# A two-block transformer kernel on one core: the first 256-column product of each one-bank quantum becomes two products of 128 columns

## The chip, the cores and the metric

The kernel runs on 1 core of one Trainium2 chip. The metric is the device time of one execution in microseconds (us), the median of the runs made.

## What is computed

The reference runs three layers over one sequence of 256 tokens of width 1024, all in float32, and returns the tokens:

- layer 1, a gated linear recurrence: `proj = rms_norm(h) @ a_w_in` (1024 by 4096, split into q, f, i, g), a recurrence over chunks of 64 frames, a gate, `@ a_w_out`, then a squared-relu MLP `relu(h @ w_up)**2 @ w_down` (1024 by 4096 and back);
- layer 2, differential attention: `kv = rms_norm(h) @ w_kv` (1024 by 2048), `q = rms_norm(h) @ w_q`, two softmaxes for each of 8 heads whose difference weighs the values, `@ b_w_out`, and a second such MLP;
- layer 3, a mixer: `z = rmsnorm(x) @ w_in_2` (2080 columns, cut into a low-rank q and kv, a rotary key and three gates), causal attention, a gated short convolution, `@ w_out_2`, a gated feed-forward of width 2816 and a last gated addition.

Every projection is a matrix product of the 256 tokens with a weight matrix. These products are nearly all of TensorE's work.

## The kernel before, in words

The program is written out by hand, engine by engine. Each engine runs its own list of instructions and waits on semaphores.

**Weights.** SyncE loads weights in parts of 128 partitions by 1024 float32 values into `w_raw` (4 buffers). ScalarE rounds each part to the float32r type in `w_hi` (line 1426, 5 slots), and VectorE writes the remainder `w_raw - w_hi` to `w_lo` (line 1993, which raises `lo_ready`). The activations are held in the same way: `xs[:, kt, 0:256]` is the rounded part of the 256 tokens for the 128 input features kt, and `xs[:, kt, 256:512]` is the remainder. `xs_b` and `us` are further buffers of that layout. One float32 product is three float32r products: high by high, remainder of x by high, and high by remainder of w.

**Units and quanta.** A unit is 256 output columns by 1024 input rows, that is two parts. A quantum is the work on one part: 4 groups of 128 input rows (`kk`) by 2 output halves (`n`) by 3 products, 24 products in all. The first eight quanta of the program have two groups of rows and so 12 products. `quantum` writes them in one of five kinds, which differ in where the sums stand in PSUM:

- `feat` (lines 644 to 665): the streams of the big projections, with some products of 512 columns;
- `direct` and `tok` (lines 676 to 678 and 695 to 697): the last pair of such a stream;
- `one_bank` (lines 682 to 684): both halves in one PSUM bank, weights stationary, tokens moving;
- `one_bank_tok` (lines 689 to 691): the same with tokens stationary and weights moving, so the result has tokens on the partitions.

**Where one-bank quanta stand.** In three places, and nowhere else:

1. the input projection of layer 1 ("the first stage"): 8 quanta of 12 products and then 28 of 24, the loop `for q in range(4, HGRN_QUANTA)`. After most of them stands a piece of the recurrence (`use`, lines 904 to 936): plain float32 products, scores of 128, 64 or 32 columns;
2. keys, values and queries of layer 2 ("the second stage"): 20 quanta of 24, `diff_quantum`, with `scores` (line 1038) and transposes (line 1046) between them;
3. the mixer's projections ("the third stage"): 12 quanta of 24, `narrow`, with the attention of layer 3 between them (lines 1205 to 1230).

Each quantum first waits for `lo_ready` of its part and, with its last product, gives the slot free (`w_used`).

A plain float32 product is one instruction of the program and two records of the trace, each with its own weight load. A float32r product is one record with one weight load. `keep_streaming` (line 826) issues plain float32 products of 256 columns to bridge a pause.

Of the kernel before, what the change touches and what calls it, by code (L numbers as in the profile page):

```python
# [17 lines left out]
P = 128  # L18
D = 1024
S = 256  # L20
# [208 lines left out]
def layered_kernel(nc, a, out):  # L229

    ctx = ExitStack()
    with ctx:
# [122 lines left out]
        ps = ctx.enter_context(nc.psum_tensor("ps", [P, 8, 512], F32))  # L355
# [244 lines left out]
        def _(pe):  # L600
            mm = nc.tensor.matmul
# [39 lines left out]
            def quantum(s, kt0, nk, last_kt, x, kind, pset, kk0=0, tiles=(0, 1), wide=0, wide_first=False):  # L641

                hi, lo = w_hi[:, s, :].rearrange("p (k n) -> p k n", k=4), w_lo[:, s, :].rearrange("p (k n) -> p k n", k=4)
                if kind == "feat":
                    steps = [(kk, n) for kk in range(kk0, kk0 + nk) for n in tiles]

                    def both_halves(some):
                        for kk, n in some:
                            o = mm(ps[:, 2 * pset + n, :], hi[:, kk, n * P:(n + 1) * P], x[:, kt0 + kk, :],  # L649
                                   start=kt0 + kk == 0, stop=kt0 + kk == last_kt)  # L650
                        return o

                    def one_half(some):
                        for kk, n in some:
                            for half in range(2):
                                at = slice(half * S, (half + 1) * S)
                                mm(ps[:, 2 * pset + n, at], hi[:, kk, n * P:(n + 1) * P], x[:, kt0 + kk, at], start=False,  # L657
                                   stop=False)
                        for kk, n in steps:
                            o = mm(ps[:, 2 * pset + n, 0:S], lo[:, kk, n * P:(n + 1) * P], x[:, kt0 + kk, 0:S], start=False,  # L660
                                   stop=False)
                        return o

                    if wide_first:
                        both_halves(steps[:wide])
                        return one_half(steps[wide:])
                    one_half(steps[:-wide])
                    return both_halves(steps[-wide:])
                for kk in range(kk0, kk0 + nk):
                    kt = kt0 + kk  # L670
                    first, last = kt == 0, kt == last_kt
                    for n in tiles:
                        bank = 2 * pset + n
                        if kind == "direct":
                            w = slice(n * P, (n + 1) * P)
                            mm(ps[:, bank, 0:S], hi[:, kk, w], x[:, kt, 0:S], start=first, stop=False)  # L676
                            mm(ps[:, bank, 0:S], hi[:, kk, w], x[:, kt, S:2 * S], start=False, stop=False)  # L677
                            o = mm(ps[:, bank, 0:S], lo[:, kk, w], x[:, kt, 0:S], start=False, stop=last)  # L678
                        elif kind == "one_bank":
                            w = slice(n * P, (n + 1) * P)  # L680
                            at = slice(n * S, (n + 1) * S)
                            mm(ps[:, pset, at], hi[:, kk, w], x[:, kt, 0:S], start=first and n == 0, stop=False)  # L682
                            mm(ps[:, pset, at], hi[:, kk, w], x[:, kt, S:2 * S], start=False, stop=False)  # L683
                            o = mm(ps[:, pset, at], lo[:, kk, w], x[:, kt, 0:S], start=False, stop=last and n == 1)  # L684
                        elif kind == "one_bank_tok":
                            xh = x[:, kt, n * P:(n + 1) * P]
                            xl = x[:, kt, S + n * P:S + (n + 1) * P]
                            at = slice(n * S, (n + 1) * S)
                            mm(ps[:, pset, at], xh, hi[:, kk, :], start=first and n == 0, stop=False)  # L689
                            mm(ps[:, pset, at], xh, lo[:, kk, :], start=False, stop=False)  # L690
                            o = mm(ps[:, pset, at], xl, hi[:, kk, :], start=False, stop=last and n == 1)
                        else:
                            xh = x[:, kt, n * P:(n + 1) * P]
                            xl = x[:, kt, S + n * P:S + (n + 1) * P]
                            mm(ps[:, bank, 0:S], xh, hi[:, kk, :], start=first, stop=False)
                            mm(ps[:, bank, 0:S], xh, lo[:, kk, :], start=False, stop=False)
                            o = mm(ps[:, bank, 0:S], xl, hi[:, kk, :], start=False, stop=last)
                return o

            def first_two(name, x, waits, mid=None):  # L700

                u, p = UNIT0[name], PAIR0[name]
                wait(pe, pair_summed, p)
                for b, k2 in ((0, 0), (0, 1), (1, 0), (1, 1), (0, 2), (0, 3), (1, 2), (1, 3)):
                    part = k2 // 2
                    if (b, k2) == (1, 0):
                        pe.wait_ge(unit_taken, HGRN_QUANTA // 2)
                    if b == 1 and k2 == 2 and mid is not None:
                        mid()
                    pe.wait_ge(lo_ready, 2 * (u + b) + part + 1)  # L710
                    if b == 0:
                        waits(2 * k2, 2)
                    o = quantum((2 * (u + b) + part) % SLOTS, 4 * part, 2, KT - 1, x, "feat", (p + b) % 2,
                                kk0=2 * (k2 % 2), wide=WIDE[2 * part + b][k2 % 2], wide_first=k2 % 2 == 0)

                    if b == 0 and k2 % 2:
                        o.then_inc(w_used, 1)
                    elif (b, k2) == (1, 3):
                        o.then_inc(w_used, 2)
# [9 lines left out]
            def split_unit(u, kt0, last_kt, x, kind, pset, between_tiles=None):  # L729

                for n in range(2):
                    if n == 1 and between_tiles is not None:
                        between_tiles()
                    for part in range(2):
                        nk = min(4, last_kt + 1 - kt0 - 4 * part)
                        o = quantum((2 * u + part) % SLOTS, kt0 + 4 * part, nk, last_kt, x, kind, pset, tiles=(n,))
                        if n == 1:
                            o.then_inc(w_used, 1)
                        elif part == 1:
                            o.then_inc(tail_done, 1)  # L740
# [224 lines left out]
            for q in range(4, HGRN_QUANTA):  # L965
                n, part = q // 2, q % 2
# [158 lines left out]
            for part in range(2):  # L1125
# [3 lines left out]
                for kk in range(4):  # L1129
                    kt = 4 * part + kk  # L1130
# [53 lines left out]
            for m in range(2):  # L1184
                if m == 1:
                    pe.wait_ge(z_dve, BY_DVE["uq3"])
                for kt in range(2):
                    s = (2 * UNIT0["ukv"] + kt) % SLOTS
                    xh, xl = (xs_s[:, 2 + kt, S * i + m * P:S * i + (m + 1) * P] for i in range(2))
# [115 lines left out]
            for b, k2 in ((0, 0), (0, 1), (1, 0), (1, 1), (0, 2), (0, 3), (1, 2), (1, 3)):  # L1305
# [6 lines left out]
                if b == 0:  # L1312
                    out2_wait(2 * k2, 2)
                o = quantum((2 * (u + b) + part) % SLOTS, 4 * part, 2, KT - 1, xs_m, "feat", (p + b) % 2,
                            kk0=2 * (k2 % 2), wide=WIDE[2 * part + b][k2 % 2], wide_first=k2 % 2 == 0)
# [1746 lines left out]
```

## Time and profile before

| | us |
|---|---|
| median of 3 runs | 964.85 |
| lowest and highest run | 964.24 and 965.42 |
| the profiled execution's own time | 964.67 |
| its span | 962.8 |
| TensorE busy in the span | 951.4 (99%), 7530 products |
| weight loads busy | 910.4 (95%), 7530 loads |
| VectorE busy | 747.8 (78%) |
| ScalarE busy | 547.8 (57%) |
| granted TensorE clock | 1.00, that is 2.4 GHz |

The span is what the trace covers; the execution's own time is 1.9 us longer. A product's record lasts from its start to the end of its results, and the next product starts well before that. So the pace of the products is read from the distance of their starts, or from the busy time of a group divided by its count, and not from the length of one record. In the tables below, PE is TensorE's product side, PEld its weight loads, DVE is VectorE, ACT is ScalarE and POOL is GpSimd.

### The profile page before, as it was taken

To read this page: it belongs to the slowest core of one execution; us is meant where nothing else is said; L and a number is where in the kernel's file an instruction comes from. 1 tells how busy PE (TensorE), PEld (TensorE's weight loads), DVE (VectorE), ACT (ScalarE), POOL (GpSimd) and SP (SyncE) were. 2 spreads that over 40 slices of the span, in tenths; PEclk is the share of its full clock that TensorE was granted. 3 is DMA by queue.
4 is the path that set the end of the run, shared out by engine and by line. 5 is a ranking of instruction groups with operands and counts; after the bars stand their busy time and mean duration, and the time that the engine had idled before them with its cause. 6 is when DMAs were issued, how large, how long until landed. Compare 5 with 4: busy or idle time off the path is not lost.

```text
span 962.8 us, 18424 instructions
## 1 busy us (share of the span) xinstructions
PE 951.4 (99%) x7530; PEld 910.4 (95%) x7530; DVE 747.8 (78%) x1129; ACT 547.8 (57%) x813; POOL 89.4 (9%) x91
## 2 busy tenths in 40 slices
PE   9999999999999999999999999999999999999998
PEld 8999999999999999999999999999999999999998
DVE  7898778978855599867987845489887998787776
ACT  6642366656454476666666534455566665556454
POOL 5334101000201000001000201001001000000000
PEclk9999999999999999999999999999999999999999
DMA  8743444766666836435566565626536366655651
GB/s 257 241 122 116 145 126 139 217 199 198 190 186 195 259 118 212 136 119 178 150 204 204 171 214 189 186 77 182 178 112 211 111 202 214 191 183 178 197 173 44
DMA packets 164723, 166.62 MB, mean 173 GB/s; under 512 B 6784, under 2 KB 162832, under 8 KB 164640
## 3 DMA queue, kind: packets, MB, share of 16 engines
q1 hardware_dynamic: 162752, 163.47, 54.6%
q0 software_dynamic: 1056, 1.19, 0.5%
q10 hardware_dynamic: 832, 0.79, 0.4%
q8 instruction: 60, 0.98, 0.4%
q14 instruction: 23, 0.19, 0.1%
HBM read 163.82 MB, written 1.08 MB: 171 GB/s over the span
## 4 chain that ended last, share of the span: by engine, by line
PE 80%; DVE 13%; issue 2%; ACT 2%; DMA 2%; SPq 0%; POOL 0%; ACTq 0%; DVEq 0%
PE ps L657 19%; PE ps L660 16%; PE ps L649 13%; DVE w_lo L1993 4%; PE ps L682 2%; PE ps L676 2%; PE ps L678 2%; PE ps L677 2%; PE ps L683 2%; PE ps L684 2%; PE ps L609 2%; PE ps L617 2%; PE ps L610 2%; PE ps L689 1%; PE ps L690 1%
## 5 line engine op out<-in xcount | busy, mean ns | idle before, releaser
L1993 DVE TENSOR_TENSOR w_lo<-w_raw,w_hi 128x1024 fp32r<-128x1024 f32 (+4 forms) x314 | 374.9, 1204 | 116.8 <-ACT w_hi L1426 111.0
L1426 ACT ACTIVATE w_hi<-w_raw 128x1024 fp32r<-128x1024 f32 x298 | 313.4, 1056 | 200.5 <-PE ps L660 47.6
L657 PE MATMUL ps<-xs,w_hi 128*128 128x256 f32 x1012 | 133.1, 277 | 0.0
L657 PEld LDWEIGHTS ps<-xs,w_hi 128*128 128x128 f32 x1012 | 127.4, 188 | 4.5
L660 PE MATMUL ps<-xs,w_lo 128*128 128x256 f32 x832 | 112.6, 277 | 0.0
L660 PEld LDWEIGHTS ps<-xs,w_lo 128*128 128x128 f32 x832 | 103.2, 188 | 0.2
L682 PE MATMUL ps<-xs,w_hi 128*128 128x256 f32 x320 | 91.4, 286 | 0.0
L683 PE MATMUL ps<-xs,w_hi 128*128 128x256 f32 x320 | 89.4, 280 | 0.0
L684 PE MATMUL ps<-xs,w_lo 128*128 128x256 f32 x320 | 89.4, 279 | 0.0
L649 PE MATMUL ps<-xs,w_hi 128*128 128x512 f32 x326 | 85.3, 393 | 0.2 <-DVE mo L2021 0.2
L1433 ACT ACTIVATE tmp<-ps 128x512 f32<-128x512 f32 x75 | 44.6, 595 | 71.2 <-PE ps L649 63.0
L657 PE MATMUL ps<-us,w_hi 128*128 128x256 f32 x626 | 81.8, 277 | 0.0
L657 PEld LDWEIGHTS ps<-us,w_hi 128*128 128x128 f32 x626 | 78.6, 188 | 2.8
L2021 DVE TENSOR_TENSOR mo<-ps,tmp 128x512 f32<-128x512 f32 x75 | 51.5, 687 | 37.8 <-ACT tmp L1433 37.8
L2971 POOL TENSOR_TENSOR sq<-sq 128x512 f32<-128x512 f32 x12 | 20.1, 1678 | 545.8 <-ACT sq L1484 375.2
L660 PE MATMUL ps<-us,w_lo 128*128 128x256 f32 x516 | 69.3, 277 | 0.0
L649 PEld LDWEIGHTS ps<-xs,w_hi 128*128 128x128 f32 x326 | 56.6, 188 | 9.9 <-DVE mo L2021 1.6
L660 PEld LDWEIGHTS ps<-us,w_lo 128*128 128x128 f32 x516 | 63.6, 188 | 0.0
L682 PEld LDWEIGHTS ps<-xs,w_hi 128*128 128x128 f32 x320 | 60.1, 188 | 0.9 <-issue 0.3
L683 PEld LDWEIGHTS ps<-xs,w_hi 128*128 128x128 f32 x320 | 60.1, 188 | 0.2
L684 PEld LDWEIGHTS ps<-xs,w_lo 128*128 128x128 f32 x320 | 60.0, 187 | 0.0
L649 PE MATMUL ps<-us,w_hi 128*128 128x512 f32 x203 | 53.4, 394 | 0.0
(431 smaller groups left out, 1892.0 us busy)
## 6 DMA issues: line engine op xcount, KB each, us to landing
w_raw<-in_mlp_w_up SPq DMA_DIRECT2D x64, 512.0 KB, 4.1
w_raw<-in_mlp_w_down SPq DMA_DIRECT2D x64, 512.0 KB, 3.7
w_raw<-in_a_w_in SPq DMA_DIRECT2D x32, 512.0 KB, 4.4
w_raw<-in_w_gate SPq DMA_DIRECT2D x22, 512.0 KB, 3.9
w_raw<-in_w_up SPq DMA_DIRECT2D x22, 512.0 KB, 4.5
w_raw<-in_w_down SPq DMA_DIRECT2D x20, 512.0 KB, 4.1
w_raw<-in_w_kv SPq DMA_DIRECT2D x16, 512.0 KB, 4.3
w_raw<-in_w_in SPq DMA_DIRECT2D x16, 512.0 KB, 4.0
```

Source lines behind the costliest of these rows:

```text
L609: mm(o_ap, hi[:, w], x[:, kt, 0:S], start=kt == 0 and (kind == "feat" or n == 0), stop=False)
L649: o = mm(ps[:, 2 * pset + n, :], hi[:, kk, n * P:(n + 1) * P], x[:, kt0 + kk, :], start=kt0 + kk == 0, stop=kt0 + kk == last_kt)
L657: mm(ps[:, 2 * pset + n, at], hi[:, kk, n * P:(n + 1) * P], x[:, kt0 + kk, at], start=False, stop=False)
L660: o = mm(ps[:, 2 * pset + n, 0:S], lo[:, kk, n * P:(n + 1) * P], x[:, kt0 + kk, 0:S], start=False, stop=False)
L682: mm(ps[:, pset, at], hi[:, kk, w], x[:, kt, 0:S], start=first and n == 0, stop=False)
L683: mm(ps[:, pset, at], hi[:, kk, w], x[:, kt, S:2 * S], start=False, stop=False)
L684: o = mm(ps[:, pset, at], lo[:, kk, w], x[:, kt, 0:S], start=False, stop=last and n == 1)
L1426: o = fn(dst, raw, ACT.Copy)
L1433: o = fn(tmp[0:rows_, pset if slot is None else slot, :, :], ps[0:rows_, 2 * pset:2 * pset + 2, S:2 * S], ACT.Copy, scale=scale)
L1993: return v.tensor_tensor(d, x, y, ALU.subtract)
L2021: return v.tensor_tensor(dst, ps[0:rows_, 2 * pset:2 * pset + 2, 0:S], tmp[0:rows_, pset if slot is None else slot, :, :], ALU.add)
L2971: g.tensor_tensor(pair(j), pair(j), pair(j - 1), ALU.add).then_inc(sq_added, 1)
```

## The change

In `one_bank` and `one_bank_tok`, the very first product of a quantum (first group of rows, half 0, high by high) is issued as two products of 128 columns, each with the same stationary operand and one half of the moving columns. The flag that opens the accumulation stands on the first of the two alone. All other products stay as they are.

```diff
                         elif kind == "one_bank":
                             w = slice(n * P, (n + 1) * P)
                             at = slice(n * S, (n + 1) * S)
-                            mm(ps[:, pset, at], hi[:, kk, w], x[:, kt, 0:S], start=first and n == 0, stop=False)
+                            if kk == kk0 and n == 0:
+                                for m in range(2):
+                                    half = slice(m * P, (m + 1) * P)
+                                    mm(ps[:, pset, half], hi[:, kk, w], x[:, kt, half], start=first and m == 0, stop=False)
+                            else:
+                                mm(ps[:, pset, at], hi[:, kk, w], x[:, kt, 0:S], start=False, stop=False)
                             mm(ps[:, pset, at], hi[:, kk, w], x[:, kt, S:2 * S], start=False, stop=False)
                             o = mm(ps[:, pset, at], lo[:, kk, w], x[:, kt, 0:S], start=False, stop=last and n == 1)
                         elif kind == "one_bank_tok":
                             xh = x[:, kt, n * P:(n + 1) * P]
                             xl = x[:, kt, S + n * P:S + (n + 1) * P]
                             at = slice(n * S, (n + 1) * S)
-                            mm(ps[:, pset, at], xh, hi[:, kk, :], start=first and n == 0, stop=False)
+                            if kk == kk0 and n == 0:
+                                for m in range(2):
+                                    half = slice(m * P, (m + 1) * P)
+                                    mm(ps[:, pset, half], xh, hi[:, kk, half], start=first and m == 0, stop=False)
+                            else:
+                                mm(ps[:, pset, at], xh, hi[:, kk, :], start=False, stop=False)
                             mm(ps[:, pset, at], xh, lo[:, kk, :], start=False, stop=False)
                             o = mm(ps[:, pset, at], xl, hi[:, kk, :], start=False, stop=last and n == 1)
```

On TensorE the program has 7203 product instructions before and 7271 after, 68 more: one for each of the 8 + 28 + 20 + 12 quanta. No other engine's list changes. In the first stage, after a piece of the recurrence, TensorE's list before reads:

```order
L684 MATMUL ps<-xs,w_lo 128x256
L936 MATMUL ps<-hq_both,hk 128x64 x8
L682 MATMUL ps<-xs,w_hi 128x256
L683 MATMUL ps<-xs,w_hi 128x256
L684 MATMUL ps<-xs,w_lo 128x256
L682 MATMUL ps<-xs,w_hi 128x256
```

and now:

```order
L689 MATMUL ps<-xs,w_lo 128x256
L946 MATMUL ps<-hq_both,hk 128x64 x8
L685 MATMUL ps<-xs,w_hi 128x128 x2
L688 MATMUL ps<-xs,w_hi 128x256
L689 MATMUL ps<-xs,w_lo 128x256
L687 MATMUL ps<-xs,w_hi 128x256
```

The first product behind the recurrence's eight is now two of half the width (line 685); line numbers behind the edit are 5 higher here, and 10 higher below both edits. Where the tokens are stationary, TensorE's list before is:

```order
L926 MATMUL ps<-hq_both,hk 32x32 x16
L689 MATMUL ps<-w_hi,xs 128x256
L690 MATMUL ps<-w_lo,xs 128x256
L691 MATMUL ps<-w_hi,xs 128x256
L689 MATMUL ps<-w_hi,xs 128x256
```

and now:

```order
L936 MATMUL ps<-hq_both,hk 32x32 x16
L697 MATMUL ps<-w_hi,xs 128x128 x2
L700 MATMUL ps<-w_lo,xs 128x256
L701 MATMUL ps<-w_hi,xs 128x256
L699 MATMUL ps<-w_hi,xs 128x256
```

Again one product of 256 columns has become two of 128 (line 697), and the rest stands as before.

## Rows read from the trace of the kernel before

**Rows 1.** The page: busy times, clock, and the chain that ended last by engine.
```profile
PE 951.4 (99%) x7530; PEld 910.4 (95%) x7530; DVE 747.8 (78%) x1129; ACT 547.8 (57%) x813; POOL 89.4 (9%) x91
...
PEclk9999999999999999999999999999999999999999
...
PE 80%; DVE 13%; issue 2%; ACT 2%; DMA 2%; SPq 0%; POOL 0%; ACTq 0%; DVEq 0%
```

**Rows 2.** Timeline of PE, first stage, 41 to 55 us: start, length, what.
```profile
41.92 1.97 PE L917 MATMUL ps<-hq_both,hk 128*128 128x128 f32 x16
43.65 0.37 PE L682 MATMUL ps<-xs,w_hi 128*128 128x256 f32 x1
...
51.74 0.28 PE L683 MATMUL ps<-xs,w_hi 128*128 128x256 f32 x1
51.86 0.28 PE L684 MATMUL ps<-xs,w_lo 128*128 128x256 f32 x1
...
52.33 1.89 PE L936 MATMUL ps<-hq_both,hk 128*128 128x64 f32 x16
54.03 0.37 PE L682 MATMUL ps<-xs,w_hi 128*128 128x256 f32 x1
54.24 0.28 PE L683 MATMUL ps<-xs,w_hi 128*128 128x256 f32 x1
54.36 0.28 PE L684 MATMUL ps<-xs,w_lo 128*128 128x256 f32 x1
```

**Rows 3.** Groups of PE by shape: count, then busy us, mean ns of one.
```profile
L826 PE MATMUL ps<-table 128*128 128x256 f32 x62 | 14.6, 381 | 0.0
L936 PE MATMUL ps<-hq_both,hk 128*128 128x64 f32 x96 | 11.4, 272 | 0.0
L917 PE MATMUL ps<-hq_both,hk 128*128 128x128 f32 x64 | 8.0, 276 | 0.9 <-DVE hq_both L2290 0.9
```

**Rows 4.** The chain, 144 to 147 us: products of 512 and of 256 columns.
```profile
144.46 1.37 PE ps L649 x6
145.84 0.91 PE ps L657 x8
```

**Rows 5.** Timeline of the weight loads at the end of rows 2.
```profile
54.01 0.19 PEld L682 LDWEIGHTS ps<-xs,w_hi 128*128 128x128 f32 x1
54.12 0.19 PEld L683 LDWEIGHTS ps<-xs,w_hi 128*128 128x128 f32 x1
54.24 0.19 PEld L684 LDWEIGHTS ps<-xs,w_lo 128*128 128x128 f32 x1
```

**Rows 6.** What PE waited for, 9 to 110 us.
```profile
PE ps L917 <- DVE hq_both L2290: 0.9, 1, 0.9
```

**Rows 7.** Timeline of PE around 36 us, between two quanta.
```profile
35.84 0.28 PE L684 MATMUL ps<-xs,w_lo 128*128 128x256 f32 x1
36.17 0.38 PE L682 MATMUL ps<-xs,w_hi 128*128 128x256 f32 x1
```

**Rows 8.** The chain, 45 to 50 us: start, us, what.
```profile
45.20 1.71 DVE hq_both L2309
46.91 0.61 DVE hq_both L2290
47.61 2.06 PE ps L917 x16
```

**Rows 9.** What PE waited for, second stage, 340 to 400 us.
```profile
PE ps L882 <- DVE rstd L2082: 0.5, 1, 0.5
...
PE ps L1038 <- DVE aq L2518: 0.3, 1, 0.3
```

**Rows 10.** The chain, second stage: its last VectorE step and what follows.
```profile
367.62 0.61 DVE aq L2518
...
368.36 1.15 PE ps L1038 x12
```

**Rows 11.** What PE waited for, third stage, 645 to 720 us.
```profile
PE ps L1230 <- ACT turned_t L1842: 0.8, 1, 0.8
...
PE ps L822 <- DVE ms L2630: 0.3, 1, 0.3
```

**Rows 12.** The chain, third stage: where it enters and leaves TensorE.
```profile
670.80 0.39 PE ps L1145
...
698.04 0.25 PE ps L1208
698.31 0.70 DVE stat L2729
```

## The prediction

> **What bounds the kernel now.** I read the page first. TensorE is busy for 99% of the span, its weight loads for 95%, at the full granted clock, 2.4 GHz, in every slice, and 80% of the chain that ended last is TensorE's [rows 1]. So an instruction more on TensorE counts in full, except where the chain runs through another engine. The busy share doesn't say what sets TensorE's own pace, product or weight load, and that is the question here. For it I read the timeline inside one stage.
>
> Within a quantum, 256-column products start 0.118 us apart [rows 2]: line 684 at 51.86 us, the end of the quantum at 52.33 us, four products later, (52.33 - 51.86) / 4 = 0.1175. Every product has its own weight load, even where the next one uses the same weights: lines 682 and 683 both take `hi[:, kk, w]`, and both have a load, 0.11 to 0.12 us apart [rows 5]. So the two new halves will have two loads, too.
>
> How the time of a product goes with its columns is seen in the streams: six products of 512 columns take 1.37 us, 0.228 each, and eight of 256 take 0.91 us, 0.114 each [rows 4]. Twice the columns, twice the time: there the columns are the limit. Below 256 columns no float32r product with 128 stationary columns occurs in this kernel. The nearest rows are plain float32. Their records of 256 columns take 14.6 / 62 = 0.235 us [rows 3], twice the 0.114 to 0.118 of a float32r product. I take it that such a record streams each column twice. Then a plain record of 64 columns streams as long as a float32r product of 128 would: half of 0.118, 0.059 us. But the sixteen records of line 936 last from 52.33 to 54.03 us, 1.70 / 16 = 0.106 us each [rows 2], and over the run 11.4 / 96 = 0.119 [rows 3]. Plain records of 128 columns, with twice the streaming, take no more: 8.0 / 64 = 0.125 [rows 3]. Something of about 0.106 us that doesn't depend on the columns is the floor. What both have, and what is the same in both, is the load of 128 by 128 weights.
>
> By the Trainium skill, "TensorE: Matmul & The Clock Gate", section "LDWEIGHTS (loading the stationary operand)", a load takes its columns divided by 1.2 GHz, 107 ns for 128 columns. The trace agrees: 0.106 us.
>
> **The change, part by part.**
>
> *The added products.* 68 quanta each swap one product of 256 columns for two of 128. Before: 0.118 us. After: two starts at the pace of the load, 2 x 0.106 = 0.212 us. The difference is 0.094 us. The upper bound: a half costs as much as a whole product does here, 0.118, as if the loads and not the columns set the pace in these quanta, difference 0.118. The lower bound, with no floor at all: two halves of 0.059, difference 0. I take 0.100, near the first: line 936 is the row with the same streaming time and the same load; the small addition is for line 917, whose sixteen records need (43.65 - 41.92) / 16 = 0.108 us each where they wait for nothing [rows 2]. 68 x 0.100 = **6.8 us** of TensorE time (between 68 x 0.094 = 6.4 and 68 x 0.118 = 8.0).
>
> *What other work hides.* In three places the chain runs through VectorE or ScalarE, and TensorE comes early and waits. First stage: until 47.61 us the chain is VectorE's [rows 8]. TensorE waits 0.9 us there [rows 6], and 0.33 instead of 0.12 us lie between two starts at 35.84 and 36.17 us [rows 7], 0.2 more. 16 quanta start before 47.61 us (8 short, then 8), 16 x 0.100 = 1.6 us, of which 0.9 + 0.2 = 1.1 go into these waits. Second stage: the chain is VectorE's until 368.36 us [rows 10], five quanta lie before it, 0.5 us, and the waits there are 0.5 and 0.3 us [rows 9], so all 0.5 is hidden. Third stage: 12 quanta; 4 of them stand before 670.80 us and 3 behind 698.31 us, where the chain is elsewhere [rows 12]. The waits of 0.3 and 0.8 us [rows 11] have room for about 7 x 0.100 = 0.7. Together 1.1 + 0.5 + 0.7 = **2.3 us hidden**; nothing if these engines wait for TensorE in turn, at most the sum of all the waits named, 3.0 us.
>
> *What queues behind.* With its last product a quantum frees a weight slot and a PSUM bank, now 0.1 us later. ScalarE and VectorE, which wait for them, are 57% and 78% busy [rows 1], and TensorE's own next wait moves by the same amount, so I cost this at nothing. Were the cover gone, the pace would still be TensorE's.
>
> *The restart.* After plain float32 records the first float32r product lasts 0.37 us instead of 0.28, and the next starts 0.21 later instead of 0.12 [rows 2]. About 40 of the 68 quanta start so. The load of that first product starts only at 54.01 us, 0.02 before its product [rows 5]. It is laid bare whatever the width of the product, so I leave it unchanged: nothing. It comes back as a rival.
>
> *The sum.* 6.8 - 2.3 = 4.5 us. The profiled execution took 964.67 us, which gives 969.2. The median of the runs lies 0.18 above it, so for the median 964.85 + 4.5 = **969.3 us**, 0.47% slower. No clock change is expected: TensorE gets no new pause. From the bounds, this case alone spans 964.85 + 6.4 - 3.0 = 968.2 to 964.85 + 8.0 = 972.9.
>
> A rule that gives another sum: the same page of the Trainium skill, section "Back-to-back issue gap", states about 81 ns for each load and product in a stream of 128-column products. By that the pair would cost 0.162, 0.044 more than before, and 68 of them 3.0 us, some 966.6 with half of it hidden. The trace speaks against it, by its 0.106 us for the shorter streaming of rows 2.
>
> **The rivals.**
>
> 1. *Half the columns, half the time* (chance 0.08). The columns are the limit everywhere, and the 0.106 us of line 936 is a cost of plain float32, two records for a product, and not of the load. For: in the streams time goes exactly with columns [rows 4]. Against: two plain records of 64 columns and two of 128 cost nearly the same [rows 3]. The time is then between 964.85 and, with a part of the load showing, 966.6. The same time results if the change doesn't do what it says, say if the two halves are put together again on the way to the chip; the order of instructions speaks against that.
>
> 2. *A short float32r product runs like plain float32* (0.12). Nowhere does this kernel use a float32r product under 256 columns, so nothing shows that the single pass holds there. Priced as plain products, two records of 0.108 us a half (line 917, above), the pair costs 4 x 0.108 = 0.43 us, 0.314 more than before. 68 x 0.314 = 21.4, less at most 3.0 hidden: 983.2 us, and 986.2 with nothing hidden. For: the difference of a factor of two in streaming between the two types shows that there are modes. Against: the order has one instruction each, and nothing in the trace ties a mode to a width.
>
> 3. *The other side: faster, through the restart* (0.03). The first product behind plain records costs 0.09 us more because its load is exposed. If a first product of half the width lets the second load and the following product start earlier, 40 quanta could each get back up to 0.09, 3.6 us, 961.3 us. The price is that a half must take at most (0.118 + 0.09) / 2 = 0.104 us in those quanta and not cost anything in the other 28. A half of 0.106 already decides against it, so this needs rival 1 to hold as well.
>
> **How the numbers follow.** The forecast has 0.74. Rivals 1, 2 and 3 have 0.08, 0.12 and 0.03, and 0.03 is left for something unforeseen, such as a longer wait elsewhere, on the slow side. A measurement of this kernel can tell about 0.2%, 1.9 us, from no change. Slower by more than that: the forecast, rival 2, the rest and none of rival 1 but its edge, 0.89. Within it: rival 1, and a little of the forecast if more is hidden, 0.08. Faster: 0.03. The range takes the forecast's 968.2 to 972.9 with a margin, 973.5, and reaches down to 965.5, into rival 1, to hold 8 in 10; rival 2 stays outside.
>
> **What would show it right or wrong.** In the new profile: 7598 products and 7598 loads. The two halves (lines 685 and 697) should start about 0.106 us apart, and the product behind them again 0.106 later. Their loads should last the 0.19 us of the others. 0.06 between the halves is rival 1, and 0.21 or more is rival 2. The wait of line 917 at 47.6 us should fall from 0.9 to near 0, and those of the second stage by about 0.5. If those waits stay and the stage ends later all the same, the engines wait for each other and nothing is hidden. If the first product of the stream behind the first stage (line 649 before) starts 2.5 us later (28 + 8 quanta, 3.6 us, less 1.1), the sum is right there. The prediction is wrong in its core if the time is under 966.5 or over 975.

## The result and the profile after

The changed kernel takes 968.09 us (median of 6 runs, 967.94 to 968.78), the kernel before 964.88 (6 runs, 964.24 to 965.61). The ratio is 1.0035, 95% interval 1.0025 to 1.0044: slower by 3.2 us. The forecast was 969.3 and slower. The profiled execution took 968.5 us with a span of 966.7, which is 3.9 us more than the span before, so the account below, made from the two traces, explains 3.9 and not 3.2.

The page of the changed kernel, the lines that answer to [rows 1]:

```profile
span 966.7 us, 18560 instructions
...
PE 957.4 (99%) x7598; PEld 916.9 (95%) x7598; DVE 748.5 (77%) x1129; ACT 547.7 (57%) x813; POOL 88.4 (9%) x91
...
PEclk9999999999999999999999999999999999999999
...
PE 87%; DVE 9%; issue 2%; ACT 2%; POOL 0%; ACTq 0%; DVEq 0%
```

68 products and 68 loads more, as the order said. TensorE is busy 6.0 us more and its loads 6.5, the other engines the same within 1 us, and TensorE's share of the chain has risen from 80% to 87%. The first-stage stretch that was VectorE's is now TensorE's.

What a split costs is seen best inside a run of quanta with nothing between them. Timeline of PE, kernel before (start, length, what), five products from the middle of the second quantum:

```profile
11.05 0.28 PE L684 MATMUL ps<-xs,w_lo 128*128 128x256 f32 x1
11.16 0.28 PE L682 MATMUL ps<-xs,w_hi 128*128 128x256 f32 x1
11.28 0.28 PE L683 MATMUL ps<-xs,w_hi 128*128 128x256 f32 x1
11.40 0.28 PE L684 MATMUL ps<-xs,w_lo 128*128 128x256 f32 x1
11.52 0.28 PE L682 MATMUL ps<-xs,w_hi 128*128 128x256 f32 x1
```

and of the changed kernel, where the second quantum begins with the two halves of line 685 (a row marked x2 holds two products):

```profile
11.01 0.28 PE L689 MATMUL ps<-xs,w_lo 128*128 128x256 f32 x1
11.12 0.34 PE L685 MATMUL ps<-xs,w_hi 128*128 128x128 f32 x2
11.30 0.34 PE L688 MATMUL ps<-xs,w_hi 128*128 128x256 f32 x1
11.47 0.28 PE L689 MATMUL ps<-xs,w_lo 128*128 128x256 f32 x1
11.59 0.28 PE L687 MATMUL ps<-xs,w_hi 128*128 128x256 f32 x1
```

Three products' worth of work took 11.52 - 11.16 = 0.36 us and takes 11.59 - 11.12 = 0.47. The product behind the halves, line 688, has a record of 0.34 us instead of 0.28: its record has started and, as the run nought shows below, it waits for its weights. So the cost lies partly behind the halves, which is why one must read from one full product to the next. The loads of the changed kernel at this place, timeline of PEld:

```profile
11.01 0.31 PEld L685 LDWEIGHTS ps<-xs,w_hi 128*128 128x128 f32 x2
11.23 0.19 PEld L688 LDWEIGHTS ps<-xs,w_hi 128*128 128x128 f32 x1
11.35 0.19 PEld L689 LDWEIGHTS ps<-xs,w_lo 128*128 128x128 f32 x1
```

The two loads of line 685 and that of line 688 start (11.23 - 11.01) / 2 = 0.11 us apart.

After a plain float32 group, where [rows 2] is the picture before, the third product began 54.36 - 54.03 = 0.33 us after the first; now the figure is 55.06 - 54.64 = 0.42. That is 0.09 more here, and 0.104 on average over the 40 splits that have other work ahead of them and lie in no wait, as against 0.105 for the 19 that follow a quantum at once.

```profile
54.64 0.42 PE L685 MATMUL ps<-xs,w_hi 128*128 128x128 f32 x2
54.89 0.33 PE L688 MATMUL ps<-xs,w_hi 128*128 128x256 f32 x1
55.06 0.28 PE L689 MATMUL ps<-xs,w_lo 128*128 128x256 f32 x1
```

I matched the third product of every group of three in both timelines, 512 of them, and so followed how late the changed kernel is at each of the 68 quanta. In 59 of the 67 steps from the end of a quantum to the third product of the next the gap grew by 0.105 us on average (by 0.107 among the first nine quanta, counted from the first third product of one to that of the next). In 8 it grew less or shrank: by 1.01 us at the 17th quantum (the use of line 917 at 47.6 us), by 0.21 and 0.22 at two others, by little at the rest. Against 0.105 for each, these 8 hide 2.5 us: 1.5 in the first stage, 0.8 in the second, 0.1 in the third. The waits that went into it: of those between 9 and 110 us the profile names none any more (before 0.9 us, [rows 6]), and in the second stage, where before there were 0.5 and 0.3 [rows 9], the row of line 892 (882 before) is left of them, with 0.2:

```profile
PE ps L892 <- DVE rstd L2092: 0.2, 1, 0.2
```

The sum, from the traces: the first product starts 0.2 us later (9.52 instead of 9.31, the work ahead of it being later in this execution); 68 x 0.105 = 7.1 us for the splits; 2.5 hidden; and 0.9 us less inside the quanta, behind their first three products. That is 3.9, and 3.96 was measured at the last quantum. The 0.9 was not in the prediction. It comes from quanta whose products now follow each other every 0.1133 us instead of every 0.1178. (The expectations below have the faster pace as 0.1136; 21 steps from 331.09 to 333.47 us in the kernel before give 0.1133.) The first quantum with stationary tokens before:

```profile
67.51 0.28 PE L691 MATMUL ps<-w_hi,xs 128*128 128x256 f32 x1
67.63 0.28 PE L689 MATMUL ps<-w_hi,xs 128*128 128x256 f32 x1
67.75 0.28 PE L690 MATMUL ps<-w_lo,xs 128*128 128x256 f32 x1
67.86 0.28 PE L691 MATMUL ps<-w_hi,xs 128*128 128x256 f32 x1
67.98 0.28 PE L689 MATMUL ps<-w_hi,xs 128*128 128x256 f32 x1
68.10 0.28 PE L690 MATMUL ps<-w_lo,xs 128*128 128x256 f32 x1
68.22 0.28 PE L691 MATMUL ps<-w_hi,xs 128*128 128x256 f32 x1
```

and after, from the third product behind the start of the quantum on, where the two halves count as one:

```profile
68.35 0.28 PE L701 MATMUL ps<-w_hi,xs 128*128 128x256 f32 x1
68.47 0.28 PE L699 MATMUL ps<-w_hi,xs 128*128 128x256 f32 x1
68.58 0.28 PE L700 MATMUL ps<-w_lo,xs 128*128 128x256 f32 x1
68.70 0.28 PE L701 MATMUL ps<-w_hi,xs 128*128 128x256 f32 x1
68.81 0.28 PE L699 MATMUL ps<-w_hi,xs 128*128 128x256 f32 x1
68.92 0.28 PE L700 MATMUL ps<-w_lo,xs 128*128 128x256 f32 x1
```

Six products took 68.22 - 67.51 = 0.71 us; now five take 68.92 - 68.35 = 0.57, 0.118 and 0.114 each. Of the 60 full quanta, 9 ended at the faster pace before and 21 do now.

### The profile page after: what moved, and what is told of

It reads as the page before. It is cut to its first block, busy times and chain, and to the rows that moved or that the text cites. A ratio compares the mean times of both kernels' runs of the same rounds, so it can differ in the third digit from the quotient of the medians.

```text
span 966.7 us, 18560 instructions
## 1 busy us (share of the span) xinstructions
PE 957.4 (99%) x7598; PEld 916.9 (95%) x7598; DVE 748.5 (77%) x1129; ACT 547.7 (57%) x813; POOL 88.4 (9%) x91
## 4 chain that ended last, share of the span: by engine, by line
PE 87%; DVE 9%; issue 2%; ACT 2%; POOL 0%; ACTq 0%; DVEq 0%
PE ps L657 19%; PE ps L660 16%; PE ps L649 13%; PE ps L688 4%; PE ps L689 4%; PE ps L687 3%; PE ps L676 3%; PE ps L677 3%; PE ps L678 3%; DVE w_lo L2003 2%; PE ps L617 2%; PE ps L609 2%; PE ps L610 2%; PE ps L700 1%; PE ps L701 1%
## 5 line engine op out<-in xcount | busy, mean ns | idle before, releaser
L657 PE MATMUL ps<-xs,w_hi 128*128 128x256 f32 x1012 | 133.1, 277 | 0.0
L657 PEld LDWEIGHTS ps<-xs,w_hi 128*128 128x128 f32 x1012 | 127.4, 188 | 4.5
L688 PE MATMUL ps<-xs,w_hi 128*128 128x256 f32 x320 | 91.7, 287 | 0.0
L687 PE MATMUL ps<-xs,w_hi 128*128 128x256 f32 x276 | 77.0, 279 | 0.0
L649 PEld LDWEIGHTS ps<-xs,w_hi 128*128 128x128 f32 x326 | 56.6, 188 | 9.7 <-DVE mo L2031 1.5
L688 PEld LDWEIGHTS ps<-xs,w_hi 128*128 128x128 f32 x320 | 60.2, 188 | 0.0
L687 PEld LDWEIGHTS ps<-xs,w_hi 128*128 128x128 f32 x276 | 51.8, 188 | 0.0
```

The lines of the kernel that those rows point to most:

```text
L687: mm(ps[:, pset, at], hi[:, kk, w], x[:, kt, 0:S], start=False, stop=False)
```

## The experiments

Each was made from the kernel before. The edits are shown shortened, for `one_bank` alone: all products that they don't name stay as they were, and `one_bank_tok` is edited in the same way, except in lead512 and lead512x4. Two questions were open: what sets the 0.106 us of an added product, and what sets the pace of the products of 256 columns.

### What an added product costs

**quarters**: four products of 64 columns in place of the first.

```diff
-    mm(ps[:, pset, at], hi[:, kk, w], x[:, kt, 0:S], ...)
+    if kk == kk0 and n == 0:
+        for m in range(4):
+            part = slice(m * 64, (m + 1) * 64)
+            mm(ps[:, pset, part], hi[:, kk, w], x[:, kt, part], start=first and m == 0, stop=False)
```

> The first product of each of the 68 one-bank quanta is issued as four of 64 columns, the same arithmetic. Theory (an added product costs one load of 128 by 128 weights, 0.106 us, whatever its columns): 3 x 0.106 = 0.318 us more a quantum than before, 68 of them 21.6 us, less about 2.5 hidden and 1 to 2 won in the pace of the later products: 982 to 984 us. Rival 1 (the change's cost is that of splitting at all, a disturbance of the pipeline of about 0.1 us a quantum, and not of each product): about the time of the change, 968. Rival 2 (the pace follows the columns, the change's 0.106 us is overhead of two fills): four fills, about 0.3 us again; the profile tells it from the theory by the distance of the four starts and of their loads, 0.106 us by the theory.

Measured: 981.01 us (ratio 1.0169, 1.0154 to 1.0185), 1 us under the range. In the first stage, outside the waits, each quantum adds 0.326 us to the lateness against the kernel before: 3 x 0.109. So the price goes with the number of products. Rival 1, a price for splitting at all, is out. A fixed price of 0.11 us for each added product, which is what rival 2 comes to, gives this sum too; the next run, corner, rules it out. The time falls short of 982 because more was hidden than I allowed: the last quantum is 17.4 us late, where 68 x 0.326 = 22.2.

**corner**: four products of 64 stationary by 128 moving columns, in 36 quanta.

```diff
+    if kk == kk0 and n == 0 and not first:
+        for m in range(4):
+            r, c = m // 2, m % 2
+            part = slice(c * P, (c + 1) * P)
+            mm(ps[0:64, pset, part], hi[:, kk, n * P + r * 64:n * P + (r + 1) * 64], x[:, kt, part], ...)
```

> In the 36 one-bank quanta that don't open a sum, the first product is issued as four of 64 stationary by 128 moving columns. Left out: the second pair of the four adds to partitions 0 to 63 instead of 64 to 127, so half of that product lands in the wrong place. Theory (the floor is the load, and the load goes with its stationary columns; line 926 before, 128x64 weights, needs 1.08 / 16 = 0.0675 us a record): 4 x 0.0675 - 0.118 = 0.152 us a quantum, 5.5 us in all, less about 1.5 hidden: 967 to 969.5 us, and four starts 0.06 to 0.07 us apart. Rival (a product has a fixed floor of 0.106 us whatever it loads): 4 x 0.106 - 0.118 = 0.306 us a quantum, 11.0 us in all, less 1.5: 973 to 975 us.

Measured: 966.89 us (1.0021, 1.0012 to 1.0030), 0.1 us under the theory's range and far from the rival's. In the first eight quanta the split ones come 0.17 to 0.18 us later. So the four together take 0.118 + 0.175 = 0.293 us, 0.073 each, less than the (0.118 + 0.107) / 2 = 0.112 of one of the change's two halves. Fewer stationary columns make a product cheaper with the same moving columns. The lines that show it, timeline of PE of this kernel in the second quantum, where the four take 11.39 - 11.14 = 0.25 us by their starts and line 690 behind them waits for its full load:

```profile
11.14 0.40 PE L686 MATMUL ps<-xs,w_hi 128*64 128x128 f32 x4
11.39 0.33 PE L690 MATMUL ps<-xs,w_hi 128*128 128x256 f32 x1
11.56 0.28 PE L691 MATMUL ps<-xs,w_lo 128*128 128x256 f32 x1
```

**every_group**: the split in every group of 128 rows (`if n == 0` in place of `if kk == kk0 and n == 0`), 256 splits.

> The high-by-high product of half 0 is split in every group of 128 rows, not in the first alone: 256 splits (60 x 4 + 8 x 2) instead of 68, the same arithmetic. Theory: 256 x 0.106 = 27.1 us, less 2.5 to 3 hidden, less what a faster pace of the later products gives back (up to 0.1 us a quantum): 983 to 989 us. Rival (only the first split of a quantum costs, because it stands where the slot and the bank change): about 968 us.

Measured: 984.01 us (1.0200, 1.0186 to 1.0213), inside the range. The three further splits in a quantum add 0.25 to 0.33 us to it in most of the 60 full quanta (0.42 at most), by its pace before and now. The rival's 968 is out: the place at the head of a quantum is not what costs.

**nought**: nothing split; a product of 32 stationary by 32 moving columns of zeros behind the first.

```diff
     mm(ps[:, pset, at], hi[:, kk, w], x[:, kt, 0:S], start=first and n == 0, stop=False)
+    if kk == kk0 and n == 0:
+        mm(ps[0:32, pset, 0:32], hi[:, kk, 0:32], nought[:, :], start=False, stop=False)
```

> Nothing is split. Instead, after the first product of each of the 68 quanta stands a product of 32 stationary by 32 moving columns whose moving operand is zeros, so that it adds nothing. By the load, 32 columns of weights cost 0.02 to 0.03 us (line 926 before: 0.63 / 32 = 0.020 us a record with 128x32). Theory (an added product costs what its load costs, not a fixed 0.106): 68 x 0.025 = 1.7 us, less most of it hidden or won back by the faster pace, which such a short product can set as the split does: 964.5 to 966.2. Rival (any added product costs 0.106 us): 7.2 us less 2.5 hidden, 969.6.

Measured: 971.63 us (1.0072, 1.0059 to 1.0085). That is far from my theory and 2 us above the rival. The theory fell here: a load of 32 columns should have cost 0.02 to 0.03 us, and through the first eleven quanta each comes 0.11 us later, as in the change. The timeline of PE of this kernel and, below it, of its loads show how:

```profile
54.45 0.36 PE L683 MATMUL ps<-xs,w_hi 128*128 128x256 f32 x1
54.65 0.18 PE L685 MATMUL ps<-nought,w_hi 128*32 128x32 f32 x1
54.68 0.36 PE L686 MATMUL ps<-xs,w_hi 128*128 128x256 f32 x1
54.88 0.28 PE L687 MATMUL ps<-xs,w_lo 128*128 128x256 f32 x1
55.00 0.28 PE L683 MATMUL ps<-xs,w_hi 128*128 128x256 f32 x1
```

```profile
54.42 0.19 PEld L683 LDWEIGHTS ps<-xs,w_hi 128*128 128x128 f32 x1
54.54 0.11 PEld L685 LDWEIGHTS ps<-nought,w_hi 128*32 128x32 f32 x1
54.66 0.19 PEld L686 LDWEIGHTS ps<-xs,w_hi 128*128 128x128 f32 x1
54.77 0.19 PEld L687 LDWEIGHTS ps<-xs,w_lo 128*128 128x128 f32 x1
```

The small load is done early and gains nothing, for the load of line 686 starts at 54.66 us, when the small product does (54.65), and not before. Line 686 then has a record of 0.36 us, 0.08 longer, and waits. So the load of a product lies behind the product just ahead of it and behind no earlier one, and a product occupies TensorE for the longer of two times: its own stream, or **the load of the product after it**. With 0.112 us for a load of 128 columns, 0.118 for 256 moving columns, and half of each for half the columns (0.056 and 0.059), the four runs fit one rule. The change: two halves, each followed by a full load, 2 x 0.112 - 0.118 = 0.106 (measured 0.107). Quarters: 4 x 0.112 - 0.118 = 0.330 (0.326). Nought: one more product followed by a full load, 0.112 (0.11). Corner: three followed by a half load, 0.059 each, and one by a full load: 3 x 0.059 + 0.112 - 0.118 = 0.171 (0.17 to 0.18). A product that takes the longer of its stream and its own load also fits the first two, but would give 4 x 0.059 - 0.118 = 0.118 in corner and 0.03 in nought. A fixed price of 0.11 for each added product fits all but corner, where three added products cost 0.175 and not 0.33.

The total of nought is 7.0 us, though, and 68 x 0.112 = 7.6, less about 2.5, gives 5. The rest is the subject of pad128 below.

### What the other engines hide

**early16** and **late52**: the change in the first 16 quanta alone, and in the other 52 alone (a counter of the quanta in `quantum`).

```diff
+    if kk == kk0 and n == 0 and one_bank_quanta[0] <= 16:   # late52: > 16
```

> The split is made only in the 16 quanta that start before 47.6 us. Theory (TensorE comes early there and waits 0.9 + 0.2 us for VectorE, so that most of the 16 x 0.106 = 1.7 us disappears in these waits): 0.3 to 0.7 us more than before, 965.2 to 965.6, and no wait of line 917 for VectorE. Rival (VectorE waits for TensorE in turn, nothing is hidden): 1.7 us more, 966.5 to 966.7, with the wait of line 917 still near 0.9 us.

> The split is made only in the 52 quanta that start after 47.6 us. Theory: 52 x 0.106 = 5.5 us, less 1.2 hidden in the second and third stage, less about 1 us of faster pace: 3.0 to 3.6 us more than before, 967.9 to 968.5, and together with the run on the first 16 the time of the change. Rival (nothing is hidden): 5.5 us less the pace, 969.3 to 970.5.

Measured: 964.99 us (0.9998, 0.9989 to 1.0007) and 967.74 us (1.0028, 1.0017 to 1.0038), that is 0.1 and 2.9 us more than before. Both are 0.2 us under the theory's lower ends, and their sum, 3.0, is near the change's 3.2. That nothing was hidden in the first 16 would have been 1.7 us and is outside the interval. In late52, where nothing is added ahead of it, the wait of the row [rows 6] is still there, in early16 it is gone. Timeline of PE of late52:

```profile
47.97 2.06 PE L933 MATMUL ps<-hq_both,hk 128*128 128x128 f32 x16 [0.87 <-DVE hq_both L2306]
```

and of early16:

```profile
48.72 2.06 PE L933 MATMUL ps<-hq_both,hk 128*128 128x128 f32 x16
```

The profiled execution of late52 has one more thing that bears on the next question. Up to its 17th quantum the instructions are those of the kernel before, in the same places in memory; even so its first eleven quanta run at 0.1133 us a product, and not at 0.1178 as in the kernel before. TensorE gains 0.05 us in each quantum of 12 products and loses it again in a wait for VectorE at the place of [rows 7]:

```profile
36.53 0.39 PE L692 MATMUL ps<-xs,w_hi 128*128 128x256 f32 x1 [1.04 <-DVE w_lo L2009]
```

### What sets the pace of the products

**tok_only**: the change only in `one_bank_tok`, 16 quanta.

> The split is made only in the 16 quanta with the tokens stationary. Their cost by the load is 16 x 0.106 = 1.7 us. Theory of two paces (after the split the later products of such a quantum often run 0.1136 us apart instead of 0.1178, 0.07 to 0.09 us a quantum given back in 10 to 14 of the 16): net 0.6 to 1.0 us, 965.5 to 965.9. Rival (no such gift: what looks like it is chance of the profiled run): 1.7 us less 0.1 hidden, 966.4 to 966.6. Since the two lie near each other, the profile decides: the distance of the starts in those 16 quanta.

Measured: 965.57 us (1.0006, 0.9998 to 1.0015). This is inside the theory's range and under the rival's, but by the time alone it can't be told from no change. In the profile, 15 of the 16 quanta end at the faster pace, against 7 before, 14 with the whole change and 15 in late52. The four other profiled runs that leave these 16 quanta and `xs` as they were have 8 (early16, lead512) and 9 (lead512x4, pad128). So the gift comes again with this split. Not every short product brings it: with four products of 64 columns (quarters) it is 7. Why, no run shows.

**split_last**: the last high-by-high product of the quantum is split instead of the first (`if kk == kk0 + nk - 1 and n == 1`).

> In each of the 68 quanta the high-by-high product of the last group and half 1 is split instead of the first, the same arithmetic. Theory of two paces (a split product can set the products behind it to the faster pace, 0.1136 us instead of 0.1178, until the next plain float32 group): little stands behind the split here, so most of that gift is lost and the time is 0.5 to 1 us above the change's, 968.6 to 969.2. Rival (the faster pace has nothing to do with the split): the same as the change, 967.9 to 968.3.

Measured: 968.81 us (1.0036, 1.0023 to 1.0049), inside the theory's range and 0.7 above the change. The intervals of the two overlap, so the time supports the theory and doesn't prove it. In the profile 12 of the 60 full quanta run at the faster pace ahead of the split, near the 9 of the kernel before, and what stands behind the split is too short to win much.

**lead512** and **lead512x4**: wide products at the head of the quantum.

```diff
-    mm(ps[:, pset, at], hi[:, kk, w], x[:, kt, 0:S], ...)
-    mm(ps[:, pset, at], hi[:, kk, w], x[:, kt, S:2 * S], ...)
+    if kk == kk0 and n == 0:             # lead512x4: if kk < kk0 + 2
+        mm(ps[:, pset, :], hi[:, kk, w], x[:, kt, :], ...)
```

> In the 52 one-bank quanta with stationary weights, the first two products (256 columns each) are one of 512 columns over the whole bank. Left out: the product with the remainder of x lands in the other half of the bank. One product of 512 columns costs 0.228 us, two of 256 cost 0.236. Theory of two paces (a product with more columns than its load needs lets the loads get ahead, and the products behind it then keep the faster pace): the other 22 products of such a quantum 0.1136 us apart, 52 x (0.09 + 0.008) = 5.1 us less TensorE work, most of it on the path: 960 to 961.5 us. Rival (the pace hangs on the stage, the bank or the neighbours on other engines and not on what TensorE did before): 0.4 us less than before, 964.3 to 964.8, and starts 0.1178 us apart.

> As the run with one product of 512 columns in front, but the first four pairs of high products of each of the 52 quanta with stationary weights are products of 512 columns, as the streams of the big projections have four to six of them in a row. Left out: each of these products' remainder half lands in the other half of the bank. Theory A (a row of several wide products brings the faster pace, a single one was too few): the products behind them start 0.1136 us apart, about 4 us less than before, 960.5 to 961.5. Theory B (the pace in these quanta doesn't hang on the products' width): starts 0.1178 us apart as before, the wide ones 0.236, time 964.5 to 965.2.

Measured: 964.98 us (0.9999, 0.9990 to 1.0008), near its rival's range, and 965.01 us (1.0004, 0.9995 to 1.0014), inside that of theory B. My theory that wide products let the loads get ahead fell twice. Behind the wide ones the starts stay 0.118 us apart, and the wide one itself takes 0.23 to 0.24, timeline of PE of lead512x4:

```profile
54.90 0.40 PE L683 MATMUL ps<-xs,w_hi 128*128 128x512 f32 x1
55.13 0.28 PE L687 MATMUL ps<-xs,w_lo 128*128 128x256 f32 x1
55.25 0.40 PE L683 MATMUL ps<-xs,w_hi 128*128 128x512 f32 x1
55.49 0.28 PE L687 MATMUL ps<-xs,w_lo 128*128 128x256 f32 x1
```

Over all of them a wide product and the one of 256 columns behind it take 0.3505 us on average; less 0.1178 that leaves 0.233 for the wide one, against 0.229 in the streams (0.228 by [rows 4]). The slower pace costs it 0.004 us, as much as it costs a product of 256 columns, where twice that would be expected of a cost per column.

**pad128**: no product added; 128 bytes free ahead of the later buffers.

```diff
         eps_sum = sb("eps_sum", [P, 1])
+        top[0] += 128
```

> Not a product is added. 128 bytes are left free where the run with the zero products had its tile of zeros, so that the buffers behind it (us, xs_b, xs_m among them) lie 128 bytes further, as they did there. Theory (the zero products cost 68 x 0.106 = 7.2 us less 2.4 hidden, 4.8, and the other 2 of the 7.0 us measured there come from the buffers' new place, seen as 0.1175 instead of 0.1136 us between products of line 677 with us): 966.5 to 967.2 us, with such a slower pace in the products that take us. Rival (the place is nothing, and the zero products cost more than the loads): 964.9 us, as before.

Measured: 967.34 us (1.0022, 1.0013 to 1.0032), 0.1 us above the theory's range and far from the rival's. So 2.3 of nought's 7.0 us are the price of its tile of zeros, which had moved the buffers behind it in the same way. One group of PE between 134 and 345 us, `direct` products that take `us`, kernel before and then pad128 (count, busy us, mean ns):

```profile
L677 PE MATMUL ps<-us,w_hi 128*128 128x256 f32 x64 | 17.7, 276 | 0.0
```

```profile
L678 PE MATMUL ps<-us,w_hi 128*128 128x256 f32 x64 | 18.0, 281 | 0.0
```

The mean record is 276 ns at the faster pace and 281 here, and the starts are 0.1178 us apart instead of 0.1133. The run has 516 `direct` products with `us`, and 516 x 0.0045 = 2.3 us. The `feat` products of 256 columns with `us` keep their 277 ns, though the buffer they read has moved by the same 128 bytes.

**xs_place**: `xs` lies 64 bytes earlier, nothing else moves. The kernel before leaves 64 bytes (`HALF_PERIOD`) free ahead of `xs` and 64 behind it; here both are behind.

```diff
-        top[0] += HALF_PERIOD
         xs = sb("xs", [P, KT, 2 * S], F32R)
-        top[0] += HALF_PERIOD
+        top[0] += 2 * HALF_PERIOD
```

> Not a product is added. The buffer xs lies 64 bytes earlier, all others stay. If the pace of the products (0.1136 or 0.1178 us for 256 columns) hangs on where the moving and the stationary operand lie against each other in memory, the pace of many quanta or streams with xs changes, by up to 4 us in all in either direction: below 961.5 or above 966. Rival (the pace comes from what stood before on TensorE alone): as before, 964.4 to 965.3, with the same quanta fast and slow as before.

Measured: 979.39 us (1.0148, 1.0132 to 1.0164), 14.4 us slower, with not one product more and well beyond the 4 us I had set as a bound. Two groups of the same stretch that take `xs`, before and then xs_place:

```profile
L657 PE MATMUL ps<-xs,w_hi 128*128 128x256 f32 x314 | 41.5, 276 | 0.0
L660 PE MATMUL ps<-xs,w_lo 128*128 128x256 f32 x272 | 37.0, 276 | 0.0
```

```profile
L656 PE MATMUL ps<-xs,w_hi 128*128 128x256 f32 x314 | 43.2, 283 | 0.0
L659 PE MATMUL ps<-xs,w_lo 128*128 128x256 f32 x272 | 38.6, 283 | 0.0
```

Four products of line 659 take 0.48 us of the chain, 0.120 each, where four of line 660 took 0.45. None of the 60 full quanta ends at the faster pace. So the pace hangs on where the operands lie in memory. That is not all of it: with all buffers in the same place the quanta with stationary tokens change pace in run after run when a split stands ahead of them, and the first eleven quanta of late52 do with nothing changed ahead. What else has a part in it stays open.

## Why the prediction was right

- **What bounds the kernel, and that an added load shows.** Right. TensorE's share of the chain rose, the clock stayed, and the price of a split was set by loads and not by columns. Rival 1 (half the columns, half the time) would have given 0 to 1.8 us, rival 2 (a short product at the plain float32 rate) about 983 us. A quantum's split costs 0.105 to 0.107 us, not 0 and not 0.314.
- **The size of it.** I took 0.100 us a split, between 0.094 and 0.118; it is 0.105 to 0.107. The sum was 6.8 us and is 7.1 to 7.3. The row I leaned on, line 936, showed the right floor, but I gave it the wrong reason: a product waits for its successor's load behind it, not for its own. For two halves both give the same, and nought shows that it isn't always so.
- **What is hidden.** I had 2.3 us, the traces show 2.5, and early16 shows the first stage's part by itself. Of the waits named, that of line 917 went as forecast, those of the second stage fell from 0.5 and 0.3 us to 0.2 and none that is listed. That the totals agree so well is luck: I had 1.1, 0.5 and 0.7 us for the three stages, and the traces show 1.5, 0.8 and 0.1.
- **The restart.** Costed at nothing, and right: with or without a plain float32 group ahead, a split costs the same, 0.104 and 0.105 us. Rival 3 (faster through the restart) needed a half to take at most 0.104 us and to cost nothing in the other quanta; a half takes 0.112, and the kernel is slower.
- **What I did not see.** The later products of a quantum. 12 more quanta end at 0.1133 us a product, which is worth 0.9 us in the profiled execution. I had both paces before me, 0.114 in [rows 4] and 0.118 in [rows 2], used the ratio of columns and did not ask why they differed. With it and the measured price of a split the 4.5 us would have been 7.1 - 2.3 - 0.9 = 3.9, as in the profiled execution; the medians differ by 3.2. The price that I had too low and the pace that I left out work against each other, which is a part of why 4.5 came no further off.
- **The signs to look for.** 7598 products and loads: right. Halves 0.106 us apart and the next again 0.106: not seen so. The records of the two halves start 0.06 us apart in 28 of the 68 quanta, the figure I had given to rival 1, and 0.14 us or more in the other 40; the product behind begins 0.11 to 0.12 us after the second half, and in the rows above it is itself 0.06 longer. The starts of short products were a bad sign to name. The loads show the 0.11, and they last the 0.19 us of the others, as forecast. The first stream product began 135.52 - 133.74 = 1.8 us later, where I had said 2.5: 0.2 for the later start and 36 x 0.105 = 3.8 for the splits, less 1.5 hidden and 0.6 through the pace.

The rule of the Trainium skill that the prediction names beside its floor ("TensorE: Matmul & The Clock Gate", "LDWEIGHTS (loading the stationary operand)") agrees with the trace: 107 ns against 106 to 112. The same page's 81 ns for each 128-column product of a stream ("Back-to-back issue gap") would have given 0.044 us a split, and 0.107 was measured, with these float32r operands. (With half of its 3.0 us hidden it makes 964.85 + 1.5 = 966.4 us, not the 966.6 I wrote.)

## What to carry to other kernels

A small product is not cheap because it is small. It must be long enough to cover the weight load of the product behind it, and if it isn't, TensorE stands for the rest of that load; here that is any product under about 0.112 / 0.118 x 256 = 240 columns ahead of 128 by 128 float32r weights, an estimate, since no width between 128 and 256 was run. Splitting, or slipping in a tiny product, costs a load, 0.11 us, even when the weights are the same and even when the tiny product's own load is short. And before an experiment that adds a buffer is believed, run the same kernel with the buffer's room left empty: a shift of 128 bytes cost 2.3 us here and one of 64 bytes 14.4, where the whole change cost 3.2.

## What was new about the hardware

- The load of a product's weights starts when the product just ahead starts (54.66 and 54.65 us in nought), so one product covers one load. A load of 128 columns needs 0.106 to 0.112 us.
- The same products of 256 columns run at 0.1133, 0.1178 or 0.120 us at the full granted clock. A shift of 128 bytes moved the `direct` products with `us` from the first to the second (2.3 us); 64 bytes of another buffer, `xs`, moved most products that read it to the third (14.4 us).
- The pace can also change inside a run of products with all buffers in place, and then holds to the end of the quantum; in late52 it differs from the kernel before with the same instructions and places. In the 16 quanta with stationary tokens the split goes with the faster pace (14 or 15 of them in three profiled runs, 7 to 9 in five without it), a wide product doesn't. In the other 44 full quanta it is 2 before and 7 with the change, but 7 in pad128 as well, where no product was added. Whether some placement gives all quanta the faster pace, which would be about 51 x 0.09 = 4.6 us by these rows (an estimate), was not tried.
